# Two-layer decode step with cross-attention: splits, taps, decode values, layer-norm buffers and sample keys in another order

## The chip, the cores and the metric

The kernel runs on one core of one Trainium2 chip. The metric is the device time of one launch in microseconds (us). Its median before the change is 1338.72 us over three runs (1336.78 to 1340.18). TensorE is called PE here, VectorE DVE, ScalarE ACT, GpSimd POOL and SyncE SP.

## What is computed

Two layers run one after the other on 256 prompt tokens and 8 sample tokens (264 columns) of width 2048. Each layer has a mixer and a cross-attention, each between norms. The reference, cut to what matters:

```python
def mixer_sublayer(x, pos, conv_ctx, lp, past):
    hn = rms_norm(x, lp["norm_mix_pre"])
    a, b_glu, g_conv, q_lat, kv_lat, k_pe, g_mla = split_in_proj(hn, lp["w_in"])
    u = a * jax.nn.sigmoid(b_glu)
    u_ext = jnp.concatenate([conv_ctx, u], axis=1)
    conv_y = causal_depthwise_conv(u_ext, lp["conv_w"], lp["conv_b"])   # width 31
    conv_out = silu(layer_norm(conv_y, ...)) * silu(g_conv)
    q = einsum("bsr,rhe->bshe", rms_norm(q_lat, lp["q_norm_g"]), lp["w_uq"])
    q_nope, q_pe = q[..., :128], rope(q[..., 128:], pos)
    c_kv, k_pe = rms_norm(kv_lat, lp["kv_norm_g"]), rope(k_pe, pos)
    if past is None:
        attn = mla_prompt_attention(q_nope, q_pe, c_kv, k_pe, w_uk, w_uv)
    else:   # 8 samples, each over 1024 cached positions (8 pages of 128) and itself
        attn = mla_sample_attention(q_nope, q_pe, c_kv, k_pe, past[0], past[1], w_uk, w_uv)
    y = concatenate([conv_out, attn * silu(g_mla)]) @ lp["w_out"]
    return x + rms_norm(y, lp["norm_mix_post"]), c_kv, k_pe, u_ext[:, -30:]

def memory_kv(mem, lp):                      # 256 memory tokens of the prompt
    mn = rms_norm(mem, lp["norm_mem"])
    return einsum(mn, lp["w_mk"]), einsum(mn, lp["w_mv"])

def cross_sublayer(x, mem_k, mem_v, lp):     # 4 heads of 128; the samples use cached
    q = rms_norm(x, lp["norm_x_pre"]) @ lp["w_xq"]    # keys and values, 256 each
    o = softmax(q @ mem_k.T * 128 ** -0.5) @ mem_v
    return x + rms_norm(o @ lp["w_xo"], lp["norm_x_post"])
```

The outputs are y for prompt and samples, and the new latents, rotary keys, convolution states and memory keys and values of both layers.

## The kernel before, in words

Weights pass in "units" of 128 output columns. A unit is a 1 MB load into one of two `stage` buffers (SP, line 404), an upper part `whi` rounded by ACT (`hi`, recorded at line 1215), a lower part `wlo` = stage − whi by DVE (`lo`, line 1781), and 48 matmuls of PE (16 blocks of 128 rows, three products each: hi·hi, hi·lo, lo·hi; lines 639 to 641, or 655 to 657 where the unit is written in parts). `stage`, `whi`, `wlo` and the PSUM bank `U` are double, so the load of unit u+2 is issued once `lo(u)` is done, and `hi(u+2)` waits until PE has finished unit u. Units of a layer are 0 to 5 (kv and q latents), 6 and 7 (rotary key), 8 to 39 (`U_HEAD` = 8, the 8 heads with four units each: value, gate, convolution gate, head gate), 40 to 43 (`U_MK`, memory keys), 44 to 59 (`U_OUT`), 60 to 63 (`U_MV`, memory values), 64 to 67 (`U_XQ`) and 68 to 71 (`U_XO`).

Every engine has its own program, written out by hand in one order; semaphores tie the five together. Nothing is scheduled at build time. So what stands ahead of a split on ACT or DVE delays the unit that PE waits for.

- Entry of layer 0: SP gives the semaphores their first credits (a `sem_inc` each), then loads units 0 and 1. ACT and DVE split these and the first rows of x (`raw_upper`, `raw_lower`), take the squares of the input rows (`row_squares`), and PE sums them (`row_factors`) between units 1 and 2. In layer 1 POOL reloads the prompt memory `memN` (2 MB, line 488) and the convolution contexts `ctxN` at the start.
- Start of the heads: the root of the q norm, four copies of the contexts and, in layer 0, the squares of the memory rows stand ahead of `hi(10)`; two scalings of `memN` (1.29 us each) ahead of `lo(10)`.
- A head: DVE computes the GLU product, 31 convolution taps (`taps`, line 1934, two accumulators), row maxima and reciprocals of the softmax (`head_max`, `head_recip`), and the gates. `head_gate` makes `mf`, for which PE's next up-projection (line 763) waits. PE turns the probabilities at line 795 (`head_turns`).
- Decode: one chunk per sample. PE turns keys from pages `cp` (`keys`, line 839), makes scores, turns the probabilities (`probs`, line 872) and sums the values (`values`, line 885, written to `HE`); `mk` parts of a memory unit and layer-norm sums lie between. Pages come in halves, one by SP and one by POOL. Four pairs of buffers `lnS` hold the layer-norm's tanh and linear parts, so chunk c+4 waits for `ln_low(c)`.
- Cross-attention: POOL loads cached keys `Kt` (512 KB each) into four buffers, samples 0 to 3 at U_XQ and 4 to 7 when PE has turned 0 to 3 (`y_keys`, line 1118); the values `Vt` follow them on POOL's queue. `hi` and `lo` of unit U_XO+1 stand ahead of the prompt's outputs `x_out`.

Of the kernel before, what the change touches and what calls it, by code (L numbers as in the profile page):

```python
# [89 lines left out]
def build(nc, A, O):  # L90
# [102 lines left out]
    lnS = [[at(f"lnS{s}{e}", [P, T], W + 20480 + 2112 * s + 1056 * e) for e in range(2)] for s in range(4)]  # L193
# [15 lines left out]
    Kt = [at(f"Kt{e}", [P, 2, MH * MD], A0 + 4096 * e) for e in range(4)]  # L209
# [4 lines left out]
    Vt = [at(f"Vt{b}", [P, 2, MH * MD], (B0, B1)[b // 3] + MH * T * 4 + 4096 * (b % 3)) for b in range(6)] + Kt[0:2]  # L214
# [49 lines left out]
    h_hi = C("h_hi", 12)  # L264
    h_lo = C("h_lo", 12)
# [25 lines left out]
    z_rdy = C("z_rdy", 1)  # L291
# [97 lines left out]
    def _(sp):  # L389
# [6 lines left out]

        for c in credited:
            sp.sem_inc(c.sem, c.first)
# [11 lines left out]
        for l in range(L):  # L410
            for j in range(6):
                col = COL_KV + P * j if j < 2 else COL_Q + P * (j - 2)
                load(l, j, j % NST, block_of(j % NST), w_in[:, ds(l * KC, KC), col:col + P])
# [28 lines left out]
            load_pages(sp, l, 6, 0)  # L442
            load_out(1)
            load_pages(sp, l, 7, 0)
# [24 lines left out]
    def _(pool):  # L469
# [13 lines left out]
        for l in range(L):  # L483

            wait_apart(pool, unit_done.sem, unit_done.at(l, 1))
            if l:
                for t in range(2):
                    pool.dma_start(memN[t][:, :], A["mem_prompt"].rearrange("a (t p) d -> p (a t) d", p=P)[:, t, :]
                                   ).then_inc(mem_again, 16)
# [25 lines left out]
            for i in range(3):  # L515
                load_up(i + 1, i * 2 + 2)
# [26 lines left out]
            def load_keys(b):  # L543
                pool.dma_start(Kt[b % 4][:, :, :], mk_d[:, ds(l * 2 + b * 2 * L, 2), :]).then_inc(km_load[b % 4], 16)

            for s in range(2 * MH - 1):
                store_rows(s)

            wait_apart(pool, unit_done.sem, unit_done.at(l, U_XQ))
            for b in range(4):  # L550
                load_keys(b)
            store_rows(2 * MH - 1)

# [4 lines left out]
            for b in range(4):  # L558

                wait_apart(pool, kT_mm.sem, kT_mm.at(l, b + 1))  # L560
                load_keys(4 + b)
                for v in (2 * b, 2 * b + 1) if b < 3 else ():
                    pool.dma_start(Vt[v][:, :, :], mv_d[:, ds(l * 2 + v * 2 * L, 2), :]).then_inc(vm_load, 16)
            for v in (6, 7):
                wait_apart(pool, kT_mm.sem, kT_mm.at(l, v - 1))
# [645 lines left out]
    def _(act):  # L1211
# [51 lines left out]
        for l in range(L):  # L1263
# [38 lines left out]
            if l == 0:  # L1302
# [5 lines left out]
                for q in range(4):  # L1308
                    raw_upper(0, q, Ahi, G_MIX, par)
# [1105 lines left out]
```

## Time and profile before

| | before |
|---|---|
| median of 3 runs | 1338.72 us |
| the profiled execution | 1344.54 us |
| its span | 1342.9 us |
| mean granted clock of PE | 0.953 |
| PE busy | 1204.6 us (90%) |
| DVE busy | 889.1 us (66%) |
| ACT busy | 637.2 us (47%) |
| mean DMA rate | 161 GB/s |

Busy shares are means over the whole span. [...] The clock is the share of full speed that TensorE was granted.

### The profile page before, as it was taken

How to read it: one execution, taken by the hardware profiler on the slowest of the kernel's cores; microseconds unless marked ns; L12 is line 12 of the kernel's file. 1: busy time of each engine (PE TensorE's matmuls, PEld its weight loads, DVE VectorE, ACT ScalarE, POOL GpSimd, SP SyncE). 2: the span in 40 equal slices, each digit the busy share in tenths (PEclk: the TensorE clock that was granted, in tenths of full speed). 3: DMA queues.
4: the chain of work that ended last, by engine and by line, in shares of the span. 5: the costliest groups of instructions: out<-in, count | busy, mean ns of one | idle time of the engine just before them, and what ended most of it. 6: DMA issues, size and time to landing. Idle time of an engine off the chain costs nothing. (4 is left out here: it accounts for less than half of the span.)

```text
span 1342.9 us, 25085 instructions
## 1 busy us (share of the span) xinstructions
PE 1204.6 (90%) x9846; PEld 1104.5 (82%) x9846; DVE 889.1 (66%) x1525; ACT 637.2 (47%) x1099; POOL 165.2 (12%) x278
## 2 busy tenths in 40 slices
PE   4889999998988899997798899999988979999883
PEld 4879999997766899995688899999976669999673
DVE  4578888889647344764567988888865653458535
ACT  4473444443536344653645444443434644446552
POOL 2200101010442000012011010101033400002200
PEclk7899999998999799999988999999989989999997
DMA  7754746564474376676356464746465635667711
GB/s 201 210 149 129 193 126 182 139 168 126 132 204 144 116 186 183 182 219 239 95 166 175 128 165 128 192 128 169 132 171 150 183 121 130 184 170 237 276 40 65
DMA packets 317544, 216.08 MB, mean 161 GB/s; under 512 B 21476, under 2 KB 300368, under 8 KB 316618
## 3 DMA queue, kind: packets, MB, share of 16 engines
q1 hardware_dynamic: 300624, 166.74, 44.8%
q0 software_dynamic: 16480, 47.73, 11.2%
q8 instruction: 72, 1.18, 0.4%
q14 instruction: 38, 0.31, 0.1%
q10 hardware_dynamic: 330, 0.11, 0.0%
HBM read 209.31 MB, written 7.15 MB: 161 GB/s over the span
## 5 line engine op out<-in xcount | busy, mean ns | idle before, releaser
L1781 DVE TENSOR_TENSOR wlo<-stage,whi 128x2048 fp32r<-128x2048 f32 x140 | 320.3, 2289 | 192.9 <-ACT whi L1215 186.6
L1215 ACT ACTIVATE whi<-stage 128x2048 fp32r<-128x2048 f32 (+2 forms) x159 | 274.6, 1730 | 343.0 <-PE U L641 276.1
L639 PE MATMUL U<-Ahi,whi 128*128 128x264 f32 x1184 | 348.2, 294 | 31.0 <-DVE wlo L1781 20.8
L640 PE MATMUL U<-Alo,whi 128*128 128x264 f32 x1184 | 341.2, 288 | 0.0
L641 PE MATMUL U<-Ahi,wlo 128*128 128x264 f32 x1184 | 340.3, 287 | 0.0
L639 PEld LDWEIGHTS U<-Ahi,whi 128*128 128x128 f32 x1184 | 229.2, 194 | 32.0 <-DVE wlo L1781 21.5
L640 PEld LDWEIGHTS U<-Alo,whi 128*128 128x128 f32 x1184 | 229.2, 194 | 0.1
L641 PEld LDWEIGHTS U<-Ahi,wlo 128*128 128x128 f32 x1184 | 227.8, 192 | 0.0
L1934 DVE SCALAR_TENSOR_TENSOR acc<-uext,cwall,acc 128x256 f32<-128x256 f32 x464 | 188.5, 477 | 0.1
L639 PE MATMUL U<-Bhi,whi 128*128 128x264 f32 x384 | 108.9, 284 | 0.0
L640 PE MATMUL U<-Blo,whi 128*128 128x264 f32 x384 | 108.8, 283 | 0.0
L641 PE MATMUL U<-Bhi,wlo 128*128 128x264 f32 x384 | 108.7, 283 | 0.0
L655 PE MATMUL U<-Ahi,whi 128*128 128x256 f32 (+1 forms) x288 | 89.3, 310 | 11.3 <-issue 9.3
L656 PE MATMUL U<-Alo,whi 128*128 128x256 f32 (+1 forms) x288 | 83.6, 290 | 0.0
L657 PE MATMUL U<-Ahi,wlo 128*128 128x256 f32 (+1 forms) x288 | 83.6, 290 | 0.0
L655 PE MATMUL U<-Bhi,whi 128*128 128x264 f32 x224 | 68.7, 307 | 7.6 <-DVE Blo L2110 3.8
L655 PEld LDWEIGHTS U<-Ahi,whi 128*128 128x128 f32 x288 | 57.3, 199 | 18.5 <-issue 12.7
L640 PEld LDWEIGHTS U<-Blo,whi 128*128 128x128 f32 x384 | 72.4, 188 | 0.0
L639 PEld LDWEIGHTS U<-Bhi,whi 128*128 128x128 f32 x384 | 72.3, 188 | 0.0
L641 PEld LDWEIGHTS U<-Bhi,wlo 128*128 128x128 f32 x384 | 72.0, 187 | 0.0
L656 PE MATMUL U<-Blo,whi 128*128 128x264 f32 x224 | 65.2, 291 | 0.0
L657 PE MATMUL U<-Bhi,wlo 128*128 128x264 f32 x224 | 65.0, 290 | 0.0
(418 smaller groups left out, 2209.4 us busy)
## 6 DMA issues: line engine op xcount, KB each, us to landing
stage<-in_w_in SPq DMA_DIRECT2D x76, 1024.0 KB, 5.9
stage<-in_w_out SPq DMA_DIRECT2D x32, 1024.0 KB, 6.2
stage<-in_w_mk SPq DMA_DIRECT2D x8, 1024.0 KB, 6.0
cp<-in_cache_kv_latent SPq DMA_DIRECT2D x64, 128.0 KB, 3.1
cp<-in_cache_kv_latent POOLq DMA_DIRECT2D x64, 128.0 KB, 3.1
stage<-in_w_mv SPq DMA_DIRECT2D x8, 1024.0 KB, 5.6
stage<-in_w_xq SPq DMA_DIRECT2D x8, 1024.0 KB, 5.8
Kt<-in_cache_mem_k POOLq DMA_DIRECT2D x16, 512.0 KB, 5.5
```

The costliest lines, as they stand in the source:

```text
L639: mm(bk[:, 0:cols], whi[:, s, w], hi[:, k, :], start=(k == 0), stop=False)
L640: mm(bk[:, 0:cols], whi[:, s, w], lo[:, k, :], start=False, stop=False)
L641: last = mm(bk[:, 0:cols], wlo[:, s, w], hi[:, k, :], start=False, stop=(k == KC - 1))
L655: mm(o, whi[:, s, w], hi[:, k, :], start=(k == 0), stop=False)
L656: mm(o, whi[:, s, w], lo[:, k, :], start=False, stop=False)
L657: last = mm(o, wlo[:, s, w], hi[:, k, :], start=False, stop=(k == KC - 1))
L1215: return A_(out, in_, ACT.Copy, scale=scale)
L1781: ins = V.tensor_tensor(wlo[:, s, :], stage[:, s, :], whi[:, s, :].bitcast(F32), ALU.subtract)
L1934: ins = V.scalar_tensor_tensor(a, uext[:, k:k + TP], w, a, ALU.mult, ALU.add)
```

## The change

It touches nothing in the arithmetic apart from the places where it is done. In the order of a layer:

1. The loads of units 0 and 1 of layer 0 stand ahead of the semaphores' credits (`h_hi`, `h_lo` get credits of their own). `raw_upper(0)` and `raw_lower(0)` stand ahead of `hi(0)` and `lo(0)`; the row squares, the root and the factors are spread behind units 0 to 2, with the first half of unit 3 ahead of the kv sums.
2. At the start of the heads `hi(10)` and `lo(10)` stand ahead of the root, the contexts and the squares. The scalings of `memN` go behind heads 2 and 3. In layer 1 POOL reloads `memN` after units 10 and 12, and `ctxN` a unit later.
3. From head 6 to head 7 `head_gate` stands behind six taps rather than fifteen, and ahead of `lo`.
4. In decode `values(n-1)` stands behind key group 3 (`keys(n, 3)`, the fourth) and ahead of group 4; `d_exp` stands ahead of the next key copies, its correction factor `d_alpha` is apart from it; the layer-norm sums are one part later or earlier; page 7 of SP stands ahead of output unit 1. At the end, `mk(15)` stands ahead of `probs(7)`, and `values(7)` behind the first four parts of output unit 44. Eight `lnS` buffers hold the tanh, the linear part is written back to `convY`, and its scaling is in two halves.
5. Sample keys have eight buffers: the first four loads stand between the stores of memory keys and values, the other four behind unit U_XQ, and value 6 right behind them. `hi(U_XO+1)` and `lo(U_XO+1)` stand between `y_keys`.

On ACT at the start of the heads of layer 0, before (`whi` is a split, `a_75` the value half of head 0, `junkM` the squares of the memory rows):

```order
L1215 ACTIVATE qsw<-HE 32x264 x4
L1255 ACTIVATE stdS<-stdS,epsv 128x264
L1215 ACTIVATE convctx<-HAB 128x480 x2
L1215 ACTIVATE convctx<-HC 128x480
L1215 ACTIVATE convctx<-HD 128x480
L1364 ACTIVATE junkM,rowq<-memN_55 128x2048
L1364 ACTIVATE junkM,rowq<-memN_56 128x2048
L1366 ACTIVATE rowq<-rowq,epsv 128x2
L1215 ACTIVATE whi<-stage 128x2048
L1215 ACTIVATE a_75<-U 128x264
L1215 ACTIVATE whi<-stage 128x2048
```

The same place of the changed kernel:

```order
L1227 ACTIVATE qsw<-HE 32x264 x4
L1227 ACTIVATE whi<-stage 128x2048
L1227 ACTIVATE a_75<-U 128x264
L1262 ACTIVATE stdS<-stdS,epsv 128x264
L1227 ACTIVATE convctx<-HAB 128x480 x2
L1227 ACTIVATE convctx<-HC 128x480
L1227 ACTIVATE convctx<-HD 128x480
L1439 ACTIVATE junkM,rowq<-memN_55 128x2048
L1439 ACTIVATE junkM,rowq<-memN_56 128x2048
L1441 ACTIVATE rowq<-rowq,epsv 128x2
L1227 ACTIVATE whi<-stage 128x2048
```

The first split and the copy of head 0 have moved ahead of seven operations; the second split still stands behind all of them.

On DVE from head 6 to head 7, before (`acc` are taps, `mf` is the gated head output that PE waits for):

```order
L1934 SCALAR_TENSOR_TENSOR acc_77<-uext,cwall,acc_77 128x256
L1934 SCALAR_TENSOR_TENSOR acc_78<-uext,cwall,acc_78 128x256
L1934 SCALAR_TENSOR_TENSOR acc_77<-uext,cwall,acc_77 128x256
L1781 TENSOR_TENSOR wlo<-stage,whi 128x2048
L1971 SCALAR_TENSOR_TENSOR sg<-tg,g_80 128x264
L1973 COPY SGD<-sg 128x8
L1975 TENSOR_TENSOR mf<-HC,sg 128x256
L1980 TENSOR_TENSOR Blo<-mf,Bhi 128x256
L1934 SCALAR_TENSOR_TENSOR acc_78<-uext,cwall,acc_78 128x256
```

And changed:

```order
L1969 SCALAR_TENSOR_TENSOR acc_77<-uext,cwall,acc_77 128x256
L1969 SCALAR_TENSOR_TENSOR acc_78<-uext,cwall,acc_78 128x256
L2006 SCALAR_TENSOR_TENSOR sg<-tg,g_80 128x264
L2008 COPY SGD<-sg 128x8
L2010 TENSOR_TENSOR mf<-HC,sg 128x256
L1810 TENSOR_TENSOR wlo<-stage,whi 128x2048
L2015 TENSOR_TENSOR Blo<-mf,Bhi 128x256
L1969 SCALAR_TENSOR_TENSOR acc_77<-uext,cwall,acc_77 128x256
```

The split now stands behind `mf`, and so do nine of the taps that stood ahead of it.

On POOL at the end of the memory units, before (stores `out_mkp` and `out_mvp`, key loads `Kt`, value loads `Vt`, numbered by buffer):

```order
L538 DMA out_mkp<-mkN 128x2x128 x4
L541 DMA out_mvp<-mvN 128x2x128 x3
L544 DMA Kt_127<-in_cache_mem_k 128x2x512
L544 DMA Kt_128<-in_cache_mem_k 128x2x512
L544 DMA Kt_129<-in_cache_mem_k 128x2x512
L544 DMA Kt_130<-in_cache_mem_k 128x2x512
L541 DMA out_mvp<-mvN 128x2x128
L556 MEMSET pm 128x512
L557 MEMSET qm 128x256
L544 DMA Kt_127<-in_cache_mem_k 128x2x512
L563 DMA Vt_137<-in_cache_mem_v 128x2x512
```

And changed:

```order
L545 DMA out_mkp<-mkN 128x2x128
L551 DMA Kt_127<-in_cache_mem_k 128x2x512
L545 DMA out_mkp<-mkN 128x2x128 x2
L551 DMA Kt_128<-in_cache_mem_k 128x2x512
L545 DMA out_mkp<-mkN 128x2x128
L548 DMA out_mvp<-mvN 128x2x128
L551 DMA Kt_129<-in_cache_mem_k 128x2x512
L548 DMA out_mvp<-mvN 128x2x128
L551 DMA Kt_130<-in_cache_mem_k 128x2x512
L548 DMA out_mvp<-mvN 128x2x128
L551 DMA Kt_131<-in_cache_mem_k 128x2x512
L551 DMA Kt_132<-in_cache_mem_k 128x2x512
```

Four keys now go between the stores; the fifth and the three after it follow unit U_XQ, and no key waits for `y_keys` any more.

The core of the diff:

```diff
@@ SP, entry and pages
+        for j in range(NST):
+            sp.dma_start(stage[:, j, :]..., w_in[:, 0:KC, COL_KV + P * j:COL_KV + P * (j + 1)]
+                         ).then_inc(stage_full[j], 16)
         for c in credited:
             sp.sem_inc(c.sem, c.first)
...
             load_pages(sp, l, 6, 0)
+            load_pages(sp, l, 7, 0)
             load_out(1)
-            load_pages(sp, l, 7, 0)
@@ POOL
-            wait_apart(pool, unit_done.sem, unit_done.at(l, 1))
-            if l:
-                for t in range(2):
-                    pool.dma_start(memN[t][:, :], ...).then_inc(mem_again, 16)
+            wait_apart(pool, unit_done.sem, unit_done.at(l, 1 + l))
...
             for i in range(3):
+                if l and i < 2:
+                    wait_apart(pool, unit_done.sem, unit_done.at(l, U_HEAD + 2 + 2 * i))
+                    pool.dma_start(memN[i][:, :], ...).then_inc(mem_again, 16)
                 load_up(i + 1, i * 2 + 2)
...
+            wait_apart(pool, stat.sem, stat.at(l, 6))
             for s in range(2 * MH - 1):
                 store_rows(s)
+                if s in (0, 2, 4, 5):
+                    load_keys((0, 2, 4, 5).index(s))
             wait_apart(pool, unit_done.sem, unit_done.at(l, U_XQ))
-            for b in range(4):
+            for b in range(4, NB):
                 load_keys(b)
             store_rows(2 * MH - 1)
+            load_values(6)
@@ PE, entry
             unit(2, 2, Ah, Al)
+            if l == 0:
+                row_factors()
+                part(3, 3, Ah, Al, 0, 8)
             sums(2, [sqq[:, c, :] for c in range(2)], 1, ...)
-            unit(3, 3, Ah, Al)
+            part(3, 3, Ah, Al, 8 if l == 0 else 0, KC)
@@ PE, decode
                 keys(n, 3)
+                values(n - 1)
+                keys(n, 4)
                 mk(2 * n - 1)
                 late()
-                keys(n, 4)
-                values(n - 1)
                 scores(n)
...
             mk(14)
+            mk(15)
             probs(NCH - 1)
-            mk(15)
-            values(NCH - 1)
...
-            outputs(1)
+            values(NCH - 1)
             for k in range(4, CC):
                 pe.wait_ge(ln_lo.sem, ln_lo.at(l, k + 1))
                 out_part(0, k, k + 1)
+            outputs(1)
@@ DVE, heads
-            V.tensor_scalar(memN[0][:, :], ...)
-            V.tensor_scalar(memN[1][:, :], ...).then_inc(mem_scl, 1)
...
+                    fresh_conv()
+                    lo(u + 4, 0)
+                    conv_gate(h, u + 3)
+                    taps(h + 1, 0, 6)
+                    head_gate(h, u + 4)
+                    lo(u + 5, 1)
+                    head_lower(h)
+                    taps(h + 1, 6, 19)
+                if h in (2, 3):
+                    memory_rows(h - 2)
@@ ACT
-            for n in range(2):
-                step(U_HEAD + n, n)
-                hi(U_HEAD + n + 2, n)
-                glu_halves(U_HEAD + n, 0, n)
+            step(U_HEAD, 0)
+            hi(U_HEAD + 2, 0)
+            glu_halves(U_HEAD, 0, 0)
             scaled_root(l, 2, 1.0 / (32 * QL))      # then contexts, memory squares
...
+            step(U_HEAD + 1, 1)
+            hi(U_HEAD + 3, 1)
+            glu_halves(U_HEAD + 1, 0, 1)
...
-                if c >= 4:
-                    act.wait_ge(ln_lo.sem, ln_lo.at(l, c - 3))
-                t, z = lnS[c % 4]
-                A_(t[:, :], convY[:, c, :], ACT.Tanh, ...)
-                A_(z[:, :], convY[:, c, :], ACT.Identity, ...)
+                A_(lnS[c][:, :], convY[:, c, :], ACT.Tanh, ...)
+                A_(convY[:, c, :], convY[:, c, :], ACT.Identity, ...)
...
             ln_scale(7)
+            ln_upper(3)
+            d_exp(7)
+            d_alpha(7)
             ln_upper(4)
-            d_exp(7)
             ln_upper(5)
@@ DVE, cross
-            lo(U_XQ + 5, 1)
...
             for b in range(3, NB):
                 y_keys(b)
+                if b == 5:
+                    lo(U_XO + 1, 1)
```

## Rows read from the trace of the kernel before

**Rows 1.** The page: busy per engine; DVE's splits: busy, mean ns | idle before, releaser.

```profile
PE 1204.6 (90%) x9846; PEld 1104.5 (82%) x9846; DVE 889.1 (66%) x1525; ACT 637.2 (47%) x1099; POOL 165.2 (12%) x278
...
L1781 DVE TENSOR_TENSOR wlo<-stage,whi 128x2048 fp32r<-128x2048 f32 x140 | 320.3, 2289 | 192.9 <-ACT whi L1215 186.6
```

**Rows 2.** Waits of PE: line, releaser: us in total, times, longest us.

```profile
PE U L639 <- DVE wlo L1781: 20.8, 4, 6.0
PE HAB L839 <- DMA cp<-in_cache_kv_latent: 14.8, 8, 3.6
PE HC L763 <- DVE mf L1975: 11.3, 2, 5.7
PE U L639 <- DVE Alo L1800: 10.2, 1, 10.2
PE HD L872 <- ACT sD L1467: 6.9, 2, 3.4
PE U L1118 <- DMA Kt<-in_cache_mem_k: 5.5, 2, 3.3
PE U L655 <- DVE Blo L2110: 3.8, 2, 1.9
PE HE L1100 <- DVE XOlo L2295: 3.6, 2, 1.8
PE HAB L1118 <- DMA Kt<-in_cache_mem_k: 2.5, 2, 2.0
```

**Rows 3.** Windows: us, busy (x) by engine, PEclk, DMA share, GB/s.

```profile
100.00:105.00 5.00, 5.00 (x25) 5.00 (x24) 4.97 (x11) 0.08 (x1) 0.00 (x0) 0.50 0.92 245
105.00:110.00 5.00, 5.00 (x36) 4.74 (x36) 4.50 (x12) 1.75 (x1) 0.00 (x0) 0.98 0.73 178
104.00:320.00 216.00, 216.00 (x1626) 205.77 (x1625) 180.52 (x356) 96.31 (x163) 13.16 (x18) 1.00 0.56 151
450.00:455.00 5.00, 5.00 (x25) 5.00 (x25) 0.46 (x2) 1.01 (x2) 0.00 (x0) 0.50 1.00 337
612.00:622.00 10.00, 7.35 (x69) 4.64 (x68) 4.09 (x8) 4.15 (x9) 5.96 (x9) 1.00 1.02 399
```

**Rows 4.** Timeline, entry: start, us, engine line op [idle <-releaser].

```profile
19.24 1.91 ACT L1215 ACTIVATE whi<-stage 128x2048 fp32r<-128x2048 f32 x1 [5.10 <-DMA stage<-in_w_in]
25.55 0.56 PE L639 MATMUL U<-Ahi,whi 128*128 128x264 f32 x1 [10.18 <-DVE Alo L1800]
44.84 0.59 PE L639 MATMUL U<-Ahi,whi 128*128 128x264 f32 x1 [4.60 <-DVE wlo L1781]
```

**Rows 5.** Timeline, start of the heads and head 0, layer 0.

```profile
99.47 0.59 PE L639 MATMUL U<-Ahi,whi 128*128 128x264 f32 x1 [5.61 <-DVE wlo L1781]
121.39 0.56 DVE L1946 TENSOR_TENSOR sS<-HE,cmask 128x384 f32<-128x384 f32 x1 [2.14 <-PE HE L782]
127.64 0.49 PE L795 MATMUL HE<-ident,sS 128*128 128x128 f32 x3
```

**Rows 6.** Timeline, start of layer 1 and of its heads.

```profile
706.41 1.91 ACT L1215 ACTIVATE whi<-stage 128x2048 fp32r<-128x2048 f32 x1 [10.62 <-DMA stage<-in_w_in]
710.70 0.59 PE L639 MATMUL U<-Ahi,whi 128*128 128x264 f32 x1 [5.96 <-DVE wlo L1781]
750.45 0.59 PE L639 MATMUL U<-Ahi,whi 128*128 128x264 f32 x1 [4.64 <-DVE wlo L1781]
```

**Rows 7.** Timeline, head 6 to head 7, layer 0.

```profile
329.93 0.42 DVE L1975 TENSOR_TENSOR mf<-HC,sg 128x256 f32<-128x256 f32 x1
341.85 0.56 DVE L1946 TENSOR_TENSOR sS<-HE,cmask 128x384 f32<-128x384 f32 x1 [3.27 <-PE HE L782]
348.88 0.49 PE L795 MATMUL HE<-ident,sS 128*128 128x128 f32 x3
```

**Rows 8.** Timeline, PE from decode to output unit 46.

```profile
448.34 5.34 PE L1022 MATMUL HAB<-OL,wuvD 128*128 128x8 f32 x32
465.48 0.39 PE L655 MATMUL U<-Bhi,whi 128*128 128x264 f32 x1 [1.51 <-DVE wlo L1781]
```

**Rows 9.** Timeline, the wait for a w_xq load in layer 0.

```profile
591.15 1.91 ACT L1215 ACTIVATE whi<-stage 128x2048 fp32r<-128x2048 f32 x1 [5.92 <-DMA stage<-in_w_xq]
```

## What the change should do to the time

> **What bounds the kernel now.** I read four views. The page's first part [rows 1] shows one engine that is nearly full: PE is busy 1204.6 of 1342.9 us, DVE 889.1, ACT 637.2. The other 138 us of PE are all that a change of order can win, beside the time in which PE runs at its lower clock. The waits of PE [rows 2] tell what ended those 138 us: a few long waits. Splits (`wlo`, `Alo`) end five waits, 31.0 us in all. Pages end 14.8 us, `mf` 11.3, the decode's `sD` 6.9, the sample keys 5.5 + 2.5, `Blo` 3.8, `XOlo` 3.6. The windows [rows 3] show what a wait costs afterwards. From 100 to 105 us, just behind the wait of 5.61 us that ended at 99.47 [rows 5], the granted clock is 0.50, that is 1.2 GHz, and PE does 25 matmuls; the long stretch of the heads, at 2.4 GHz (1.00), does 1626 in 216 us, 7.5 per us or 37.6 per 5 us. The 5.5 us from 99.5 to 105 thus lose 5.5 x (1 - 25/37.6) = 1.8 us. I book 2 us behind each of the long waits: the four for `wlo` of unit splits, the two for `mf`, and the decode's two tails. The wait of 5.96 us in layer 1 [rows 6] and the 5.34 us of the small products at 448.34 (0.50 in the window 450 to 455) [rows 3, 8] are of the same kind.
>
> The Trainium skill ("TensorE: Matmul & The Clock Gate", section "What's actually happening") states that the throttled clock is the default and that activity releases it. By that rule a removed wait gives back its slow stretch too, and one that arises elsewhere pays it again. The trace agrees: 0.50 behind the wait at 99.47, 1.00 over the heads without a wait [rows 3]. A sum of the waits alone, without that rule, would be -44 in place of -58.
>
> The last view is the timeline around each wait [rows 4 to 9]. It says what the waiting is for, and above all how far behind PE the next engine is, which decides how much of a removed wait stays removed. In the heads DVE is busy 180.52 of 216 us [rows 3]: an engine with 16% of slack can take over only part of the bound.
>
> **The change part by part**, each against the profiled execution.
>
> Entry of layer 0. The weights of unit 0 land at 19.24 and PE starts at 25.55 [rows 4]. The loads are issued earlier, but other inputs fill the DMA engines then, so I let unit 0 land at the same time. `raw_upper(0)` and `raw_lower(0)` ahead of the splits: 19.24 + 1.91 for `whi` and 2.29 for `wlo` [rows 1] gives 23.4, 23.5 with the hand-over, so the first product comes 2.0 us earlier. The rest of the raw rows comes while PE is at the lower clock. Row squares, root and factors go behind units 0 to 2, so the wait of 4.60 us ahead of unit 2 [rows 4] goes, its slow stretch (2.0) with it, and 0.7 us of factors that stood in the way. Sum -9.3. Bounds: -6 if the later root makes `sums` wait, -11 if unit 0 lands earlier too.
>
> Start of the heads, layer 0. `hi(10)` and `lo(10)` ahead of root, contexts and squares take away the wait of 5.61 us [rows 5] and 2.0 of slow clock: PE alone would be at 127.64 - 7.6 = 120.0 at the turns of head 0. DVE's chain is not as fast. `hi(11)` still stands behind the squares, so `lo(11)`, the GLU product and 19 taps move by 0.4 only. What DVE gains is its own wait of 2.14 us for the scores [rows 5], and some 0.8 that the turns waited for PE: 127.64 - 3.3 = 124.3. So a new wait of 4.3 us stands at the turns and a new slow stretch of 2.0 behind it: net -1.3. Bounds 0 and -5.6 (no slow stretch, and DVE through 2.3 us sooner, by the two memory scalings that went).
>
> Start of layer 1. The reload of 2 MB of memory rows stands beside the weight loads, and ACT waits 10.62 us for the load at 706.41; PE then waits 5.96 at 710.70 [rows 6]. The reload moves into the heads, where the DMA share is 0.56 [rows 3]. Wait and slow stretch go: -8.0. Bounds -5 and -9. Start of its heads: the wait of 4.64 at 750.45 [rows 6] and 2.0 go, and by the same working as in layer 0, but with no squares ahead of `hi(11)`, DVE gives back 2.4: -4.2. Bounds -2 and -6.
>
> Head 6 to 7, both layers. PE waits 11.3/2 = 5.65 for `mf` [rows 2], whose instruction starts at 329.93 [rows 7]. Nine taps and a split (2.3) move behind it, so `mf` is ready about 1.0 after PE stops: -4.7, and -2.0 for the clock. PE then reaches head 7's scores ahead of DVE, which idles 3.27 us there now [rows 7] and has the moved taps still to do; I let it take back 1.4 of the 6.7: -5.3 at the turns (348.88 to 343.6). Twice that is -10.6. Bounds -4 and -6 each.
>
> Decode, middle. The waits for pages (14.8 in eight [rows 2]) stay; they are late because pages share the queues with weight loads. `values` ahead of group 4 must now have the turned probabilities a group sooner: about 1 us lost where DVE is late. What `d_exp` ahead of key copies gives (a part of the 6.9 us behind `sD`) pays for it: 0, bounds +4 and -3 per layer.
>
> Decode, tail. Of the waits between 430 and 466 us go, in each layer, 6.9/2 = 3.4 behind `sD` and 3.8/2 = 1.9 behind `Blo` [rows 2], 1.5 ahead of unit 46 [rows 8], and 2.6 of slow clock behind them: 9.4 if all goes. `mk(15)` ahead of `probs(7)` and `values(7)` behind four parts of unit 44 give PE work of their own during the exponentials; but DVE has the whole of `ln_silu`, `ln_low` and `d_norm` to finish for it. The small products at 448.34, 32 in 5.34 us, stay at whatever clock they meet. I take -7.0 per layer, -14.0 in all. Bounds -9.4 and -4 each.
>
> Cross-attention. With eight key buffers and the loads ahead, the key waits go: (5.5 + 2.5)/2 = 4.0 per layer, with 0.7 of slow clock, and the 1.8 ahead of the outputs (`XOlo`, 3.6/2) [rows 2], as one split no longer stands there. Against it stands the DMA. At 612 to 622 us the share is 1.02 at 399 GB/s [rows 3], and the load of the split at 591.15 was already 5.92 us late beside four keys [rows 9], though PE shows no long wait for it. I book +1.0 for a late unit: -5.5 per layer, -11.0. Bounds -6.5 and -2.5 each.
>
> The Trainium skill ("DMA: Bandwidth & Descriptors", section "Issuing engines are not separate DMA queues") says that DMAs of the sync, scalar and gpsimd engines run on the same 16 engines and interleave. It speaks against moving POOL's keys in front of SP's weights; by it the keys' time is not won but moved. The trace agrees in the late load of [rows 9]. The bytes are the same, so the sum keeps only the 1.0 above; by the rule at its full weight the 4.0 per layer comes back in later weights, and the sum is -50.4.
>
> The eight `lnS` buffers and the halved scaling have no price on PE by themselves; they run on ACT and DVE, which idle about half of the decode. If that cover is gone they show in the tail's bound.
>
> Sum: -9.3 - 1.3 - 8.0 - 4.2 - 10.6 + 0 - 14.0 - 11.0 = -58.4. 1344.5 - 58.4 = 1286.1 for a profiled execution, which stood 5.8 us above the median of the runs; so 1280 for the median.
>
> **The rivals.**
> First, the waits come back on DVE. For it speaks DVE's 16% of slack in the heads [rows 3] and the new wait of 4.3 us at the turns that I already have; against it, DVE itself waits 192.9 us for ACT's splits [rows 1], and these come sooner. Then the heads, the tail and the start of layer 1's heads give half (-15 of -30), entry, layer 1's start and cross-attention keep 25 of 28, the decode's middle costs +4: about -36, 1303 for the median.
> Second, all waits named go and none comes: the 31.0 of splits without the 8.2 that the first weights need, 11.3, 6.9, 3.8, twice 1.5, 3.6 and 8.0 are 59.4; eight slow stretches of 2.0 (one each at the entry, at layer 1's start and at the two starts of heads, two from head 6 to 7, two in the tails) make 75.4, so 1263.
> Third, slower: weights late behind keys, values and pages, in units 60 to 71 of both layers (24 units). The price of one late unit is that of [rows 6]: 5.96 us of wait and 2.0 of slow clock, 8 us. It turns the sign when 58.4/8, so more than seven of the 24 units, are late by that much. With ten late the time is 1280 + 80 = 1360. Against it: four keys beside weights caused no PE wait of that size before; [rows 2] has none for a w_xq load.
> Fourth, the change does not do what it says at the entry and the tail, because PE's order there has other waits (the first weights at 19.24, the wait for `mfd`): those two give a third, 1280 + 6 + 9 = 1295. It lies inside the range.
>
> **How the numbers follow.** Forecast (1270 to 1290) 0.45; the waits come back or parts fail (1290 to 1310) 0.30; all go (below 1270) 0.14; slower 0.04; the rest, 0.07, lies between 1310 and the time before, with 0.03 of it within 0.3% (4 us, about what a measurement of this kernel can tell from no change). So faster 0.93, same 0.03, slower 0.04. The favourable bounds add up to -81 (1257), the others to -26 (1313); they will hardly all be met together, so the range is 1260 to 1308.
>
> **What would show it.** In the changed profile: PE's waits behind `wlo` fall from 20.8 to below 6 us and the one of 10.18 to about 8; `mf` from 11.3 to about 2; no key wait; a new wait at the turns of head 0 of about 4 us with 0.50 clock behind it; the heads of a layer end about 5 us sooner from head 6 on than their start; PE's busy time falls by about 15 us with the clock. The prediction is wrong in its heads if `mf` goes but the turns do not move, in its tail if new waits of the same total stand in front of unit 44, and in its sign if `whi` waits for loads in units 60 to 71.

## The result, and the profile after

The changed kernel takes 1275.27 us (median of four, 1273.52 to 1278.11) where the kernel before takes 1339.45 (median of four beside it): the ratio is 0.9524, with a 95% interval of 0.9498 to 0.9549. That is 64 us, or 4.8%, less. The forecast was 1280, with a range of 1260 to 1308. The profiled execution went from 1344.5 to 1275.5, which is 69 us: the profile before was one of the longer runs, so the difference of the two profiles is some 5 us more than that of the medians.

The page of the changed kernel, with busy time per engine and the granted clock in 40 slices (each digit is tenths of full speed):

```profile
PE 1186.9 (93%) x9846; PEld 1089.3 (86%) x9846; DVE 888.9 (70%) x1527; ACT 637.2 (50%) x1099; POOL 164.7 (13%) x278
...
PEclk8998999999999899999989999999999989999997
```

PE does the same 9846 matmuls in 17.7 us less of busy time [rows 1]: that part is clock, from a mean of 0.953 to 0.974. The rest, about 51 us, is idle time of PE that has gone. Its waits, to be read against [rows 2] (line, releaser: us in total, times, longest; "issue" is a wait for which the profile shows no releaser; L649 was L639, L665 was L655, L851 was L839, L775 was L763, L1130 was L1118; `pD` are the turned probabilities as DVE copies them, `sqs` is ACT's copy of partial sums):

```profile
PE U L649 <- issue: 8.0, 1, 8.0
PE U L665 <- DVE wlo L1810: 6.1, 5, 2.2
PE HAB L851 <- DMA cp<-in_cache_kv_latent: 3.2, 2, 1.7
PE U L665 <- DVE Blo L2155: 3.0, 2, 1.5
PE ST L689 <- ACT sqs L1227: 2.5, 2, 1.3
PE HC L775 <- DVE mf L2010: 2.0, 2, 1.0
PE U L649 <- DVE wlo L1810: 1.8, 3, 1.2
PE HE L897 <- DVE pD L2100: 1.8, 2, 0.9
PE HE L793 <- DVE qpr L1903: 1.6, 1, 1.6
PE HAB L851 <- issue: 1.6, 1, 1.6
PE U L1130 <- issue: 1.2, 2, 0.6
```

Two lines of the kernel before that [rows 2] leaves out belong beside them:

```profile
PE U L655 <- DVE wlo L1781: 4.7, 5, 1.5
PE HD L872 <- ACT sD L1469: 1.6, 2, 0.8
```

The 20.8 us behind `wlo` of whole units are 1.8. But unit 3 is now written in parts and counts at the other line, and with the parts it is 25.5 before and 7.9 after. `mf` went from 11.3 to 2.0, the pages from 14.8 to 3.2 (4.8 with the one whose end the profile does not explain), and the 8.0 for sample keys are gone; the 1.2 of "issue" at L1130 stood there before as well. The waits for the decode's `sD`, 6.9 and 1.6, are gone too, and 1.8 for `pD` and 2.5 for `sqs` are new. At the entry 8.0 of 10.18 remain.

By stage, from the start times of PE's work in the two timelines (us; layer 0, then layer 1 where there are two; the last column is measured less forecast):

| stretch | before | after | measured | forecast | off |
|---|---|---|---|---|---|
| launch to turns of head 0 | 127.6 | 115.7 | -11.9 | -10.6 | -1.3 |
| heads 0 to 6 | 188.2, 188.2 | 188.2, 188.2 | 0 | 0 | 0 |
| turns 6 to first keys of decode | 35.2, 36.1 | 30.5, 30.5 | -4.7, -5.6 | -5.3 each | +0.3 |
| decode, first keys to probabilities 7 | 86.4, 87.1 | 80.1, 78.6 | -6.3, -8.5 | 0 | -14.8 |
| probabilities 7 to memory-value rows | 129.0, 129.1 | 125.0, 126.6 | -4.0, -2.5 | -7.0 each | +7.5 |
| to the first U_XO product | 70.8, 71.6 | 63.4, 65.8 | -7.4, -5.8 | -5.5 each | -2.2 |
| to the turns of head 0, layer 1 | 140.4 | 126.9 | -13.5 | -12.2 | -1.3 |

The rows of the table add up to 70.2 us; from the first U_XO product of layer 1 to the end it is 1.2 us more than before (54.4 against 53.2).

Rows behind this table. First the entry and the start of the heads, to be read against [rows 4, 5] (start, length, engine, line, operation, and in brackets the idle time before with its releaser):

```profile
17.72 1.91 ACT L1227 ACTIVATE whi<-stage 128x2048 fp32r<-128x2048 f32 x1 [1.29 <-DMA stage<-in_w_in]
22.17 0.56 PE L649 MATMUL U<-Ahi,whi 128*128 128x264 f32 x1 [8.01 <-issue]
104.17 0.46 PE L793 MATMUL HE<-kvS,qnS 128*128 128x128 f32 x2 [1.64 <-DVE qpr L1903]
```

Then head 6 to 7, decode and tail, against [rows 7, 8]:

```profile
313.79 1.13 PE L775 MATMUL HC<-kvT,wuk 128*128 128x256 f32 x4 [0.99 <-DVE mf L2010]
331.32 0.55 PE L807 MATMUL HE<-ident,sS 128*128 128x128 f32 x3 [0.59 <-ACT sS L1227]
367.54 0.73 PE L851 MATMUL HAB<-ident,cp 128*128 128x128 f32 x5 [1.59 <-issue]
419.74 0.39 PE L665 MATMUL U<-Bhi,whi 128*128 128x264 f32 x1 [1.50 <-DVE Blo L2155]
```

The product for `mf` comes 0.99 us late, as forecast (1.0), and the turns of head 7 follow at 331.32, 27.4 us behind those of head 6 where it was 33.1.

Last the decode of layers 0 and 1, from the first keys to the probabilities of chunk 7, before and after, and the place of the low clock in layer 0 before (us, PE busy (x), PEclk, DMA share, GB/s):

```profile
351.00:437.39 86.39, 72.71 (x793) 0.97 0.51 149
1001.84:1088.97 87.13, 72.70 (x792) 0.98 0.51 146
334.30:414.40 80.10, 73.03 (x804) 1.00 0.60 172
948.39:1027.02 78.63, 72.98 (x804) 1.00 0.61 175
385.00:389.00 4.00, 4.00 (x25) 0.57 0.72 217
```

PE is idle for 13.7 and 14.4 us before and for 7.1 and 5.6 after. Behind the wait for the page of chunk 3 (3.42 us, 3.60 in layer 1) the clock before was low for some 3.4 us; in this profile of the changed kernel it is 1.00 throughout (runs 4, 8, 10 and 12 have 3.4 us of low clock at another place of layer 0's decode).

### The profile page after: what moved, and what is told of

The parts are those of the page before. It is cut to its first block and busy times, and to the rows that moved or that the text cites. A ratio compares the mean times of both kernels' runs of the same rounds, so it can differ in the third digit from the quotient of the medians.

```text
span 1273.8 us, 25083 instructions
## 1 busy us (share of the span) xinstructions
PE 1186.9 (93%) x9846; PEld 1089.3 (86%) x9846; DVE 888.9 (70%) x1527; ACT 637.2 (50%) x1099; POOL 164.7 (13%) x278
## 5 line engine op out<-in xcount | busy, mean ns | idle before, releaser
L649 PE MATMUL U<-Ahi,whi 128*128 128x264 f32 x1152 | 334.4, 290 | 9.8 <-issue 8.0
L650 PE MATMUL U<-Alo,whi 128*128 128x264 f32 x1152 | 328.5, 285 | 0.0
L651 PE MATMUL U<-Ahi,wlo 128*128 128x264 f32 x1152 | 328.0, 285 | 0.0
L649 PEld LDWEIGHTS U<-Ahi,whi 128*128 128x128 f32 x1152 | 219.3, 190 | 10.9 <-issue 8.2
L650 PEld LDWEIGHTS U<-Alo,whi 128*128 128x128 f32 x1152 | 219.5, 191 | 0.0
L651 PEld LDWEIGHTS U<-Ahi,wlo 128*128 128x128 f32 x1152 | 218.1, 189 | 0.0
L649 PE MATMUL U<-Bhi,whi 128*128 128x264 f32 x384 | 108.9, 284 | 0.0
L665 PE MATMUL U<-Ahi,whi 128*128 128x256 f32 (+1 forms) x320 | 96.8, 303 | 11.1 <-issue 9.3
L666 PE MATMUL U<-Alo,whi 128*128 128x256 f32 (+1 forms) x320 | 91.0, 284 | 0.0
L667 PE MATMUL U<-Ahi,wlo 128*128 128x256 f32 (+1 forms) x320 | 90.9, 284 | 0.0
L665 PEld LDWEIGHTS U<-Ahi,whi 128*128 128x128 f32 x320 | 61.4, 192 | 17.0 <-issue 11.4
L665 PE MATMUL U<-Bhi,whi 128*128 128x264 f32 x224 | 68.1, 304 | 8.2 <-DVE wlo L1810 5.2
L649 PEld LDWEIGHTS U<-Bhi,whi 128*128 128x128 f32 x384 | 72.3, 188 | 0.0
## 6 DMA issues: line engine op xcount, KB each, us to landing
cp<-in_cache_kv_latent POOLq DMA_DIRECT2D x64, 128.0 KB, 3.0
cp<-in_cache_kv_latent SPq DMA_DIRECT2D x64, 128.0 KB, 2.9
```

The costliest lines, as they stand in the source:

```text
L649: mm(bk[:, 0:cols], whi[:, s, w], hi[:, k, :], start=(k == 0), stop=False)
L650: mm(bk[:, 0:cols], whi[:, s, w], lo[:, k, :], start=False, stop=False)
L651: last = mm(bk[:, 0:cols], wlo[:, s, w], hi[:, k, :], start=False, stop=(k == KC - 1))
L665: mm(o, whi[:, s, w], hi[:, k, :], start=(k == 0), stop=False)
L666: mm(o, whi[:, s, w], lo[:, k, :], start=False, stop=False)
L667: last = mm(o, wlo[:, s, w], hi[:, k, :], start=False, stop=(k == KC - 1))
```

## The experiments

Each but the last two changes one thing of the changed kernel. "Span" compares the profiled executions (1273.8 us for the changed kernel). The ratios are to the kernel before, on the same chip. There is one profile of each kernel, and a stage that two kernels share does not take the same time in both. From the first unit's product to the turns of head 0 it is 91.4 to 94.0 us in the nine kernels that do not differ there, from U_XO to the turns of head 0 of layer 1 126.6 to 127.6, decode to the probabilities of chunk 7 158.7 to 160.0 in both layers together, and the tail 124.9 to 128.0. A difference within such a spread is not shown by one profile.

**1. Values late.**

```diff
                 keys(n, 3)
-                values(n - 1)
                 keys(n, 4)
                 mk(2 * n - 1)
                 late()
+                values(n - 1)
                 scores(n)
```

> The changed kernel with values(n-1) of a decode chunk moved back behind key group 4, the memory part and the late sums. Theory A (values release page buffers: page n may only be loaded once values(n-3) is done, so earlier values load pages earlier): from chunk 4 on the pages come late again, PE's waits for cp rise from 3.2 us to about 12 to 15 us in both layers, decode is 4 to 8 us longer per layer, the whole 8 to 14 us above the changed kernel's 1275. Rival B (values were only moved off the wait for the turned probabilities, pages are late by contention alone): the waits for cp stay near 3 us, the whole within 3 us of 1275.

1287.59 us, ratio 0.9622 (0.9596 to 0.9649), clearly above the changed kernel's interval. The profiled execution is the shortest of the four, 1283.24 us. In it decode to the probabilities 7 grows by 3.4 us in each layer. But the pages do not come late:

```profile
PE HAB L851 <- ACT KT L1227: 3.8, 12, 0.5
PE HAB L851 <- DMA cp<-in_cache_kv_latent: 3.3, 2, 1.7
PE ST L689 <- ACT sqs L1227: 5.2, 2, 2.6
```

The wait for `cp` is 3.3 us, as in the changed kernel. In its place PE waits twelve times, 3.8 us in all, for ACT's copy of the keys, and 2.7 us more for the partial sums. The wait of 0.9 us per layer for `pD` is gone. So theory A had the whole time (12 us more by the medians, 8 to 14 expected) but less than its 4 to 8 us per layer in decode, and its mechanism was wrong; rival B was right on the waits for `cp` and wrong on the time. `values(n-1)` between key groups 3 and 4 is work for PE while ACT empties the bank into which group 4 is turned.

This run does not bring back the order before. There a memory part and the sums stood between the two groups, and the kernel before has no wait for `KT` at this line; this run leaves nothing between them. So the 3.4 us are what it costs to take all work away there. What the change gained by putting values in place of the memory part no run shows.

**2. Pages late.**

```diff
             wait_apart(eng, do_mm.sem, do_mm.at(l, n - 2))
+            if n > 3:
+                wait_apart(eng, ds_mm.sem, ds_mm.at(l, n - 1))
```

> The changed kernel with PE's order untouched, but pages 4 to 7 released by scores(n-2) as well, so about as late as in the kernel before. Theory A (only the time of the page's release counts): the same loss as with values moved back, waits for cp 12 to 15 us, 8 to 14 us above 1275. Rival B (the place of values in PE's order counts, not the pages): within 3 us of 1275, cp waits near 3 us.

1280.28 us, ratio 0.9546 (0.9517 to 0.9575), which overlaps the changed kernel's. Decode grows by 0.9 and 0.7 us. The `cp` waits are 3.4 us and 2.9 more of "issue", 6.3 together; in kernels with the changed decode they are 4.5 to 6.1. So the release is worth 1.6 us at most, little more than the spread. It explains neither the loss of run 1 nor the 10 us by which the pages' waits fell.

**3. Exponentials late.** On ACT, chunks 1 to 6 (chunk 4 is shown):

```diff
-            d_exp(4)
             kt_evac(5, 0)
+            d_exp(4)
+            d_alpha(4)
             act.wait_ge(st_conv, l * 32 + 32)
             act.wait_ge(z_rdy.sem, z_rdy.at(l, 1))
             ln_scale(0)
-            d_alpha(4)
```

> The changed kernel with each decode exponential of ACT behind the first key copy of the next chunk, and its correction factor right behind it, as before the change (chunks 1 to 6). Theory A (what the exponential's place gave is what lets values stand early): PE waits for sD or pD in each chunk, 3 to 6 us per layer, whole +6 to +12. Rival B (the place of values alone gave the gain, ACT has slack): decode within 1 us per layer.

1279.47 us, ratio 0.9555 (0.9530 to 0.9580). Decode grows by 0.9 and 1.9 us, 161.5 in both layers where the spread ends at 160.0; `sD` is waited for twice, 1.7 us, in front of the probabilities of chunk 4, as before the change (1.6). Between the two theories, and nearer to B in the times. The exponential of chunk 7, behind which the 6.9 us stood, is not touched here.

```profile
PE HD L884 <- ACT sD L1484: 1.7, 2, 0.8
```

**4. The first sum late.**

```diff
-            chunk(2, late=lambda: squares_sum(0))
-            chunk(3, late=lambda: squares_sum(1))
+            chunk(2)
+            chunk(3, early=lambda: squares_sum(0), late=lambda: squares_sum(1))
```

> The changed kernel with the first half of the layer-norm's sum of squares back at the front of decode chunk 3, rather than at the end of chunk 2. The page of chunk 3 can only be issued once values(0) is done, and PE waited 3.42 us for it before the change and about 1.6 after. Theory A (the sum was moved into that wait, so that it costs nothing there): PE waits 0.7 to 1.2 us longer for the page and decode grows by as much, with up to 2 us more where the longer wait brings a low clock; whole +2 to +6. Rival B (the wait shrank by something else): within 1 us in decode.

1277.46 us, ratio 0.9567 (0.9531 to 0.9602), inconclusive. Decode changed by +0.2 and +1.3 us. The waits for pages did not grow (3.6 us `cp` and 1.3 "issue", against 3.2 and 1.6). So theory A is not borne out, but the run doesn't refute it either. In layer 0 a wait of 1.92 us before chunk 2 was followed by 3.4 us of low clock, so PE came later to page 3 and waited only 0.36 us. In layer 1 it waits 0.95 us for it, where kernels that keep the sum's place wait between 0 and 2.05.

The timelines say where a part of the wait of 3.42 us for page 3 went. Page 3 is issued as chunk 2 starts, and chunk 3 starts 11.24 and 11.44 us later before, 11.09 and 9.42 after. Of that PE spends 7.8 us in chunk 2 before, without the wait for the page, and 9.5 after: the sum (0.5, 9.5 against 9.0 in layer 1 of this run) and the new wait for `pD` (0.9) now lie in front of the page's wait. So in layer 0 the page comes as late as before, and 1.7 us of its wait are taken up by what now lies ahead of it.

**5. Head 6 to 7 as before.** The DVE branch of the diff ahead of the prediction is taken back.

> The changed kernel with DVE's order from head 6 to head 7 as before. Theory A (DVE takes back a part, the rest is the order): turns(6) to turns(7) 33 us rather than 27.4 in both layers, PE waits for mf 11 us rather than 2, whole +10 to +13 us. Rival B (the pages of the first decode chunks come late instead and hide the gain): turns as in A, but the first keys of decode follow sooner, whole +5 us or less.

1289.92 us, ratio 0.9620 (0.9602 to 0.9639). Turns 6 to 7 take 33.7 and 34.0 us, the first keys follow 2.1 us later rather than 3.0: +5.3 and +5.6 net. PE waits 11.3 us for `mf`, the number of [rows 2]. Theory A, though the median is 14.7 us above the changed kernel's rather than 10 to 13.

```profile
PE HC L775 <- DVE mf L2010: 11.3, 2, 5.7
```

**6. Reload at the start of layer 1.**

```diff
-            wait_apart(pool, unit_done.sem, unit_done.at(l, 1 + l))
+            wait_apart(pool, unit_done.sem, unit_done.at(l, 1))
+            if l:
+                for t in range(2):
+                    pool.dma_start(memN[t][:, :], ...).then_inc(mem_again, 16)
```

(and the reloads between the head weights out.)

> The changed kernel with the reload of the memory rows (2 MB) and the contexts of layer 1 back at the start of layer 1. Theory A (the reload makes weight loads late): PE waits about 6 us for a split near unit 3 of layer 1, 2 us of low clock behind it, whole +7 to +9 us. Rival B (the start of layer 1's heads hides it, since DVE is the bound there): PE's wait comes, but turns(0) of layer 1 is less than 4 us later.

1284.81 us, ratio 0.9584 (0.9545 to 0.9623). One wait comes back, and turns 0 of layer 1 are 6.7 us later. Theory A, with 4.2 us of wait rather than 6:

```profile
676.86 0.59 PE L649 MATMUL U<-Ahi,whi 128*128 128x264 f32 x1 [4.17 <-DVE wlo L1810]
```

**7. Start of the heads as before.** `step`, `hi` and `glu_halves` of the first unit go back behind root, contexts and squares on ACT, `lo(U_HEAD + 2, 0)` next to `lo(U_HEAD + 3, 1)` on DVE.

> The changed kernel with hi and lo of unit U_HEAD+2 back behind root, contexts and squares (ACT) and behind the q norm (DVE); the scalings of the memory rows stay in the heads. Theory A (PE's wait of 5.6 us was mostly hidden behind DVE's later bound in layer 0): +1 to +3 us in layer 0, +3 to +5 in layer 1, whole +4 to +8. Rival B (wait and clock come back whole): +6 to +8 per layer, whole +12 or more.

1283.13 us, ratio 0.9568 (0.9533 to 0.9602). The wait is there again, 4.82 us of it in layer 0, but the stretch from the first unit's product to the turns is only 2.1 us longer, and that of layer 1 1.5; by the spreads above it is 1.6 to 4.2 and 0.8 to 1.8. Theory A in layer 0; its 3 to 5 us in layer 1 did not come. DVE's chain is the likely bound behind it (4.93 of 5 us busy, windows of run 11).

```profile
91.44 0.39 PE L649 MATMUL U<-Ahi,whi 128*128 128x264 f32 x1 [4.82 <-DVE wlo L1808]
```

The rest of this kernel's loss (span 1283.9) is 3.0 and 1.4 us in the tails, whose code is untouched; see the last section.

**8. Factors between units 1 and 2 again.** Row squares, root, diagonal and `row_factors()` go back there on ACT, DVE and PE; raw rows and loads stay.

> The changed kernel with the row squares, root and factors of layer 0 back between units 1 and 2 on ACT, DVE and PE; the raw rows and the first loads stay as changed. Theory A (this wait of 4.6 us and its low clock were most of the entry's gain): turns(0) 5.5 to 7.5 us later, whole +6 to +8. Rival B (DVE bounds the start of the heads, so what PE loses at the entry is hidden there): turns(0) less than 3 us later.

1283.28 us, ratio 0.9591 (0.9569 to 0.9613). The wait is back in full, yet the stretch from the first unit's product to turns 0 grows by 3.6 us only, between the two expectations: DVE hides a part.

```profile
41.48 0.59 PE L649 MATMUL U<-Ahi,whi 128*128 128x264 f32 x1 [4.61 <-DVE wlo L1804]
```

**9. Credits ahead of the first loads.** The two loads of SP move behind the loop of `sem_inc`.

> The changed kernel with the first two weight loads issued behind the semaphores' credits again. Theory A (the DMA engines were full, so the time of issue matters little): whole 0 to +1 us. Rival B (the loads were late by issue): unit 0 lands at 19.2 rather than 17.7 us, first unit product 1.5 us later, whole +1.5 to +3 us.

1277.15 us, ratio 0.9529 (0.9490 to 0.9568): no difference. The loads are issued at 9.23 rather than 2.73 us, and ACT takes them at 18.01 rather than 17.72:

```profile
18.01 1.91 ACT L1227 ACTIVATE whi<-stage 128x2048 fp32r<-128x2048 f32 x1 [1.09 <-DMA stage<-in_w_in]
```

Theory A. In the one profile before, the same load from 9.40 landed at 19.24 [rows 4]; over the profiles of the changed kernel and of the twelve runs ACT takes it between 17.72 and 19.34. So the landing time is spread between executions, and no edit can be shown to move it.

**10. Keys issued as before,** into eight buffers:

```diff
-                if s in (0, 2, 4, 5):
-                    load_keys((0, 2, 4, 5).index(s))
...
-            for b in range(4, NB):
+            for b in range(4):
                 load_keys(b)
...
+            for b in range(4):
+                wait_apart(pool, kT_mm.sem, kT_mm.at(l, b + 1))
+                load_keys(4 + b)
```

> The changed kernel with eight key buffers, but the loads of sample keys and values issued where the kernel before issued them (0 to 3 behind U_XQ, 4 to 7 as y_keys go). Theory A (the early issue removes the key waits): from the memory value rows to the first U_XO product it takes 68 us rather than 63.4 in layer 0, key waits of PE 8 us again, the whole +8 to +10 us. Rival B (the early issue costs weight loads as much as it gives): within 3 us, and PE's wait of 2.21 us for a split in layer 1 goes.

1291.12 us, ratio 0.9629 (0.9611 to 0.9647). The stretch to U_XO is 71.6 and 72.2 us, so +8.2 and +6.4: theory A, with more than its +8 to +10 in all. The wait of 2.21 us for a split in layer 1 falls to 0.81, so the early keys cost about 1.4 us once, of which rival B made too much.

```profile
PE HAB L1130 <- DMA Kt<-in_cache_mem_k: 14.3, 4, 5.5
```

The key waits are 14.3 us and not the 8.0 of the kernel before. One reason lies in the changed kernel: it counts the keys' loads in pairs (`km_load[b // 2]`), so PE waits for both of a pair, where before it waited for one. In layer 0 key 6 has landed at 594.5 us, and PE turns it at 598.4, when key 7 is there. So this run costs more than the early loads alone gave.

**11. Squares later.** The squares of the memory rows leave the start of the heads:

```diff
-            if l == 0:
-                ...
-                for t in range(2):
-                    A_(junkM[:, :], memN[t][:, :], ACT.Square, ...)
-                A_(rowq[:, 4:6], rowq[:, 0:2], ACT.Sqrt, ...)
...
                 head_upper(h)
+                if l == 0 and h < 2:
+                    memory_squares(h)
```

> The changed kernel with the squares of the memory rows of layer 0 moved from the start of the heads behind heads 0 and 1 (their scratch in another place; the root there costs two more table loads of 1.28 us on ACT). Theory A (at the start of the heads DVE waits 2.5 us for the split behind the squares, and its chain ends PE's wait of 1.64 us and the low clock from 105 to 112 us): turns(0) 2 to 4 us earlier, whole -2 to -4 us. Rival B (the low clock there comes from the small products between units, not from the wait): turns(0) 1 to 2 us earlier with the clock near 0.57 again, whole -1 to -2. Rival C (ACT's longer stretch behind head 0 delays a split): 0 or slower.

1273.92 us, ratio 0.9507 (0.9473 to 0.9540), overlapping the changed kernel's interval. In the profile (span 1269.9) turns 0 come 4.1 us earlier, at 111.6; PE's wait of 1.64 us and the low clock there are gone, which speaks for theory A and against B. Windows of the changed kernel and then of this one (columns as in [rows 3]):

```profile
100.00:105.00 5.00, 3.36 (x26) 2.94 (x25) 4.93 (x10) 2.19 (x2) 0.00 (x0) 1.00 0.15 37
105.00:110.00 5.00, 5.00 (x20) 4.02 (x20) 4.93 (x13) 0.00 (x0) 0.00 (x0) 0.57 0.62 173
110.00:115.00 5.00, 5.00 (x34) 5.00 (x34) 4.93 (x13) 1.79 (x6) 0.00 (x0) 0.75 0.14 36
```

```profile
100.00:105.00 5.00, 5.00 (x35) 4.09 (x33) 4.93 (x14) 2.19 (x2) 0.00 (x0) 1.00 0.75 206
105.00:110.00 5.00, 5.00 (x44) 5.00 (x43) 4.90 (x11) 0.99 (x4) 0.00 (x0) 1.00 0.03 7
110.00:115.00 5.00, 4.04 (x34) 3.83 (x34) 4.97 (x13) 3.54 (x6) 0.00 (x0) 1.00 0.75 203
```

**12. A candidate.** Run 11's edit, and ACT's `partial(l, 4)` ahead of `d_exp(3)`.

> The changed kernel with the squares of the memory rows behind heads 0 and 1 (as in the run before) and, in each layer, ACT's copy of the partial sums ahead of exponential 3, so that PE's sum at the front of chunk 4 finds it. Theory A (both waits are real): turns(0) 4 us earlier, PE's wait of 1.26 us for sqs gone in both layers, 1269 to 1271 us. Rival B (the wait for sqs only becomes one for the page or the key copies of chunk 4): 1272 to 1274.

1275.60 us (1267.54 to 1275.85, five runs), ratio 0.9514 (0.9488 to 0.9541): no measurable gain over the changed kernel. The wait for `sqs` is gone and turns 0 come 2.9 us earlier. In layer 1 a wait of 1.11 us for the page of chunk 5 stands in its place: rival B for the sums. In layer 0 no such wait comes, but the wait in front of chunk 3 is 2.05 us rather than 1.59, 3.4 us of low clock follow it, and the tail takes 1.6 us more; these two lie in the spread of the executions.

## Why the prediction was right, and where its steps were not

The median came within 5 us of the forecast, and the profiled execution, whose kernel before ran long, within 11 (1275.5 against 1286.1). Of the mechanisms most were right. In decode they were not: counted where the forecast booked them, the middle gained 10.7 us where nothing was expected, and the tail 10.6 of 14.0. That the second error takes back a part of the first is luck.

- Entry and first heads: forecast -10.6, measured -11.9. The first product came 3.4 us earlier rather than 2.0; from the landing of its weights to it are 4.45 us (22.17 - 17.72) rather than 6.31 (25.55 - 19.24), so the edit gave 1.9 and the landing, which is spread (run 9), the other 1.5. That a removed wait is not won whole at the start of the heads was right: the wait of 4.8 us costs 2.1 at the turns (run 7), that of 4.6 at the entry 3.6 (run 8), so the forecast's split (-9.3 and -1.3) was too steep. But DVE was not the only bound: with ACT's squares out of the way too, the turns come 4.1 us earlier still (run 11). The replacing wait was not at the turns, 4.3 us long, but 1.64 us earlier in the chain, for the rotated query; a low clock followed it as forecast (0.57 and 0.75).
- Start of layer 1 and its heads: forecast -12.2, measured -13.5. Run 6 gives the reload 6.7 and run 7 the heads 1.5, of the 8.0 and 4.2 booked. Taken back one at a time the parts give 8.2 of 13.5; what the rest belongs to was not separated.
- Head 6 to 7: forecast -10.6, measured -10.3, undone +10.9. The step was right: `mf` late by 1.0, then DVE as the bound, which took back 0.6 us at the turns (0.59 in front of 331.32) and 0.9 before the first keys, 1.4 booked.
- Decode's middle: forecast 0, measured -14.8. The step that failed is "The waits for pages (14.8 in eight [rows 2]) stay": they fell by 10.0 us, to 4.8. The 3.4 us of low clock behind the longest of them in each layer went with it, 1.7 us per layer, which the step had not booked. Of what was booked, "about 1 us lost where DVE is late" came true: the new wait for `pD`, 0.9 us per layer. The whole adds up. Pages give -10.0, `sD` -8.5 (the 6.9 were booked in the tail, but end in this stretch), the clock -3.4; the new waits for `pD` and `sqs` cost 4.3, and `mk(15)`, which has moved into the stretch, twice 1.4: -14.8. Why the pages' waits fell is known in part. Of page 3's wait 1.7 us are taken up in chunk 2 (run 4), and the later release costs 1.6 us at most (run 2). Values' place (run 1) and the exponentials (run 3) bring none of it back. Page 7, whose waits of 1.29 and 1.89 us are gone, stands ahead of output unit 1 on SP; that was not tried alone.
- Decode's tail: forecast -14.0, measured -6.5. Of the waits in the term only `sD` went, and it counts in the middle's stretch. `Blo` still costs 1.5 us per layer of 1.9, and unit 46 waits 1.5 as before: from the probabilities of chunk 7 on, PE is idle for 3.9 us before and 3.8 after. So the step that lets `Blo`'s 1.9 and unit 46's 1.5 go failed, and the measured -4.0 and -2.5 are the 1.4 us of `mk(15)` that moved out, and clock. The tail takes 126.5 us in the mean of the 26 tails of thirteen profiles (124.9 to 128.0), which is 1.1 less than 129.0 - 1.4. With the 6.9 of `sD`, and without the 2.8 that `mk(15)` took out, the tail's own changes gave 10.6, and the middle's 10.7. No run takes the tail's order or the eight `lnS` buffers back, so what made `sD` go is not shown. Middle and tail together are -21.3 against -14.0.
- Cross-attention: forecast -11.0, measured -13.2; undone +14.6 (run 10). The key waits were all won, and as run 10 costs more than they gave, its 14.6 is an upper bound. That early keys make weights late shows once, in the 2.21 us of layer 1 (0.81 in run 10); it did not take the gain.

The parts undone one by one in the kernel's old order (runs 3, 5 to 8) cost about 2.8, 10.9, 6.7, 3.6 and 3.6 us in the stages that they touch, and the early keys up to 13.2 (run 10): some 41 of the 70 us that the stages gained. Run 1 doesn't count among them, since its order is that of neither kernel. The rest, mostly decode, is spread over parts that were not undone alone, or gained twice over, where either of two edits would have done.

The slower rival did not happen: no unit from 60 to 71 waits longer than 2.21 us for its weights.

## What to carry over

Before booking a removed wait, look at how idle the next engine is in the same stretch: where DVE was full (start of the heads) a wait of 4.8 us was worth 2.1 (1.6 to 4.2 by the spread), and where only weights were late (start of layer 1) one of 4.2 was worth 6.7, clock included. Where an engine alternates two banks with an engine that copies them out, keep a piece of independent work between two turns: leaving none cost 3.4 us a layer here (run 1). Ask of a run that takes a part back whether its order is really the old one; runs 1 and 10 were not. And a removed wait of 1 to 2 us ahead of a transfer can come back as a wait for the transfer, as in layer 1 of run 12.

## What the runs showed of the hardware

The same tail, from the probabilities of chunk 7 to the memory-value rows, takes close to 125.0, 126.6 or 128.0 us in kernels that do not differ there. PE is idle for 3.8 us in each of them, and the clock makes the difference. Windows over the start of the tail, for the changed kernel (125.0):

```profile
420.00:425.00 5.00, 4.64 (x33) 4.43 (x33) 2.46 (x3) 0.00 (x0) 0.00 (x0) 0.81 0.09 18
425.00:430.00 5.00, 5.00 (x24) 5.00 (x25) 0.45 (x2) 1.74 (x3) 0.00 (x0) 0.51 0.95 290
430.00:435.00 5.00, 5.00 (x43) 5.00 (x43) 0.00 (x0) 0.75 (x1) 0.00 (x0) 1.00 0.22 95
```

and of run 7 (128.0), PE alone (us, PE busy (x), PEclk, DMA share, GB/s):

```profile
423.00:428.00 5.00, 4.64 (x23) 0.50 0.00 0
428.00:433.00 5.00, 5.00 (x25) 0.50 1.00 308
433.00:438.00 5.00, 5.00 (x30) 0.64 0.22 95
```

A mean of 0.81 between the levels 0.5 and 1 means 1.9 of 5 us at the low one. So the changed kernel spends 1.9 + 4.9 = 6.8 us at 1.2 GHz there, run 7 5.0 + 5.0 + 3.6 = 13.6; half of the difference is 3.4 us, and 3.0 were measured. The low clock there follows a wait of only 1.5 us and the small products of 8 columns. It also followed the wait of 1.64 us and small products at 104 us, which I had expected of long waits alone. With that wait gone (run 11) the clock there stays at 1.00, and the small products are still there.
